# The scan of a gated linear-attention layer on one core: first inverse with swapped sides, one centred output, channel sums moved

## What is computed

```python
def step(S, inp):
    d_t, k_t, v_t, kk_t, a_t = inp[:5]
    sa = jnp.einsum("bhvk,bhk->bhv", S, -kk_t)
    S = (S * d_t[:, :, None, :] + sa[..., None] * (kk_t * a_t)[:, :, None, :]
         + v_t[..., None] * k_t[:, :, None, :])
    out = jnp.einsum("bhvk,bhk->bhv", S, inp[5]) if emit else None
    return S, out
...
kk = kk * lax.rsqrt(jnp.sum(kk * kk, axis=-1, keepdims=True) + 1e-12)
...
o = (o - mean) * lax.rsqrt(var + GN_EPS)
o = o * ln_g + ln_b
bonus = jnp.sum(r * k_sum * r_k, axis=-1, keepdims=True) * v
y = (o + bonus) * jax.nn.silu(g)
```

## Time and profile before

| | |
|---|---|
| median of 3 runs | 2918.58 us (2914.32 to 2923.76) |
| the profiled execution | 2924.89 us |
| its span, mean clock of TensorE | 2923.1 us, 0.95 |
| PE busy in the span | 2625.3 us, 90% |
| the scan within the span | about 1118 to 1830 us |
| a pair of steps in the middle of the scan | 80.6 to 87.4 us |

### The profile page before, as it was taken

One profiled execution on the slowest core, in us unless ns is written; L12 is line 12 of the kernel. 1 busy time (PEld: TensorE's weight loads), 2 busy tenths in 40 slices (PEclk: granted clock), 3 DMA queues, 4 the chain that ended last, 5 costly groups with the idle time before them and its releaser, 6 DMA issues. The chain is left out here.

```text
span 2923.1 us, 66756 instructions
## 1 busy us (share of the span) xinstructions
PE 2625.3 (90%) x28836; PEld 2002.2 (68%) x28836; DVE 1514.2 (52%) x2665; ACT 1133.3 (39%) x1779; POOL 748.4 (26%) x436
## 2 busy tenths in 40 slices
PE   7998899979899996888888887989999999898987
PEld 5776588747678785777777776767788655476745
DVE  4734578883652213545555554334540366515995
ACT  4633332242452433444444443234422344423333
POOL 2423200002212125545544440112223200041201
PEclk9999899999789897999999999989999999998998
DMA  4224344233444431111111100542312100144431
GB/s 153 87 72 134 134 112 127 69 122 113 161 151 146 173 137 57 42 47 47 44 45 53 40 5 25 207 151 65 115 58 80 58 1 1 53 136 141 136 89 58
DMA packets 83663, 266.38 MB, mean 91 GB/s; under 512 B 11824, under 2 KB 12848, under 8 KB 82992
## 3 DMA queue, kind: packets, MB, share of 16 engines
q1 hardware_dynamic: 74160, 236.97, 25.4%
q10 hardware_dynamic: 9216, 25.17, 2.2%
HBM read 203.04 MB, written 36.70 MB: 82 GB/s over the span
## 5 line engine op out<-in xcount | busy, mean ns | idle before, releaser
L373 PE MATMUL ps<-h_parts_conv,w_parts_one 128*128 128x512 f32 x3168 | 581.0, 344 | 16.1 <-DVE h_parts_conv L359 13.6
L373 PEld LDWEIGHTS ps<-h_parts_conv,w_parts_one 128*128 128x128 f32 x3168 | 496.1, 191 | 105.4 <-DVE h_parts_conv L359 15.9
L373 PE MATMUL ps<-scratch_scan 64*64 64x64 f32 (+1 forms) x15936 | 371.4, 233 | 85.2 <-issue 47.9
L373 PEld LDWEIGHTS ps<-scratch_scan 64*64 64x64 f32 x15936 | 332.6, 135 | 130.3 <-issue 99.1
L441 POOL TENSOR_TENSOR w_parts_rwkv_out<-ring,w_parts_rwkv_out 128x1024 fp32r<-128x1024 f32 x78 | 186.4, 2391 | 788.5 <-ACT w_parts_rwkv_out L370 788.5
L441 POOL TENSOR_TENSOR w_parts_one<-ring,w_parts_one 128x1024 fp32r<-128x1024 f32 x82 | 207.3, 2529 | 679.6 <-ACT w_parts_one L370 679.4
L370 ACT ACTIVATE scratch_scan<-ps 128x384 f32<-128x384 f32 x560 | 241.2, 493 | 346.2 <-PE ps L373 201.0
L367 DVE SCALAR_TENSOR_TENSOR scratch_conv<-scratch_conv,vec 128x256 f32<-128x256 f32 (+1 forms) x656 | 330.2, 578 | 0.2
L373 PE MATMUL ps<-h_parts_attn,w_parts_rwkv_out 128*128 128x512 f32 (+1 forms) x1536 | 328.6, 373 | 0.0
L373 PEld LDWEIGHTS ps<-h_parts_attn,w_parts_rwkv_out 128*128 128x128 f32 x1536 | 264.0, 189 | 58.1 <-issue 10.2
L370 ACT ACTIVATE w_parts_rwkv_out<-ring 128x1024 fp32r<-128x1024 f32 x104 | 109.6, 1056 | 368.2 <-PE ps L373 340.9
(11 more groups left out here) (218 smaller groups left out, 3368.0 us busy)
## 6 DMA issues: line engine op xcount, KB each, us to landing
ring<-in_weights SPq DMA_DIRECT2D x311, 512.0 KB, 3.8
rwkv_spill<-scratch_conv ACTq DMA_DIRECT2D x64, 384.0 KB, 2.3
stream<-rwkv_spill SPq DMA_DIRECT2D x64, 384.0 KB, 3.7
scratch_conv<-scratch_conv SPq DMA_DIRECT2D x128, 103.1 KB, 2.2
scratch_conv<-scratch_conv SPq DMA_DIRECT2D x128, 67.4 KB, 2.0
x_spill<-stream SPq DMA_DIRECT2D x2, 3072.0 KB, 11.6
y_spill<-scratch_scan SPq DMA_DIRECT2D x8, 384.0 KB, 2.8
scratch_rwkv_out<-y_spill SPq DMA_DIRECT2D x8, 384.0 KB, 6.4
```

Of the source, the lines that this page charges most:

```text
L373: return nc.tensor.matmul(o, l, r, start=start, stop=stop)
```

## The change

- A is made with swapped sides: `first_inverse(w)` forms the 64x64 products anew from AR and XX, 24 products that use all four pairings of partition halves, into the banks of both halves h at once. The identity is no longer added on PE. `p_start` multiplies by one of two triangular masks and then adds the identity in two more DVE instructions; these signal `p_started`, on which P(0), T(0) and `inverse_update` now wait.
- RD is gone. ACT copies RC into YT (two copies) and squares from there (two squares), `out_square`; it first waits for the store of YT of the pair before (`y_out`). `normal_out` is one multiply of YT in SBUF.
- PE's order: BO goes between WU(1) and Q(0); RC (even steps) and KS (odd steps) between NP and Q(1); RS behind VT. FILLS is written anew to match.
- DVE: `bonus_values` goes from behind link 7 to behind `decayed_a`. ACT: `kk_square` and its logarithms go to either side of the copies of T(1), `out_square` behind them, `out_log` and `out_inverse_root` ahead of the copies of T(3).

```diff
-            def first_inverse(w, e):
-                for n in range(6):
-                    pe.wait_ge(*read_at("G", w, n))
-                room_for(pe, "A", w, e)
-                o = bank3(fill_bank("A", w, e))
-                for par in range(2):
-                    mm(o[HS[par]], idh(par), identb[HS[par]], True, False)
-                for j in pairs_of(e):
-                    for h in range(2):
-                        for par in range(2):
-                            last = mm(o[HS[par], 2 * (j - 3 * e) + h, :], XX[HS[par], aa_plane(w), j, 0, h, :], idh(par),
-                                      False, (j, h) == (3 * e + 2, 1))
-                last.then_inc(*done_inc("A", w, e))
+            def first_inverse(w):
+                for h in range(2):
+                    room_for(pe, "A", w, h)
+                o = [bank3(fill_bank("A", w, h)) for h in range(2)]
+                for j in range(HALFC):
+                    for par in range(2):
+                        for h in range(2):
+                            last = mm(o[h][HS[par], j, :], AR[w % 3][HS[h], 2 * j + par, 0, :], XX[HS[h], bk_plane(w), j, 0, par, :])
+                            if (j, par) == (HALFC - 1, 1):
+                                last.then_inc(*done_inc("A", w, h))
...
             def p_start(w):
+                for h in range(2):
+                    v.wait_ge(*done_at("A", w, h))
+                    vtt(PQ[w % 2][:, h::2, :], bank3(fill_bank("A", w, h)), first_mask(w % 2)).then_inc(*read_inc("A", w, h))
+                for h in range(2):
+                    v.wait_ge(*read_at("A", w, h))
+                    vtt(PQ[w % 2][:, h::2, :], PQ[w % 2][:, h::2, :], identb, ALU.add).then_inc(p_started, 1)
+
+            def normal_out(i):
+                v.wait_ge(rt_ready, i + 1)
+                vtt(YT, YT, RT).then_inc(gained, 1)
...
+            def out_square(i):
+                if i > 0:
+                    a.wait_ge(y_out, 16 * i)
+                for e in range(2):
+                    a.wait_ge(*done_at("RC", i, e))
+                    act(YT[:, cols(e)], PS[:, fill_bank("RC", i, e) * 512:fill_bank("RC", i, e) * 512 + HALFC * CH],
+                        ACT.Copy).then_inc(*read_inc("RC", i, e))
+                for e in range(2):
+                    a.wait_ge(*read_at("RC", i, e))
+                    act(SQ[:, cols(e)], YT[:, cols(e)], ACT.Square).then_inc(out_squared, 1)
...
                 T(0)
                 at(w_and_u, "WU", p, 1)
+                both(bonus_sums, "BO")
                 Q(0)
...
                 at(own_values, "NP", p)
+                both(centred, "RC")
+                both(kk_sums, "KS")
                 Q(1)
```

More of the change, by code:

```diff
@@ L1918, in inv_t @@
                 if lv == 0:
-                    for h in range(2):
-                        pe.wait_ge(*read_at("A", w, h))
+                    pe.wait_ge(p_started, 2 * (w + 1))
                 if n > 2:
@@ L2084, in scan_tensor @@
                 both(values, "VT")
-                both(kk_sums, "KS")
+                both(square_sums, "RS")
                 chain(p, 5)
@@ L2092, in scan_tensor @@
                 chain(p, 7)
-                both(centred("RC"), "RC")
-                both(bonus_sums, "BO")
                 both(p_turned(4), "P4")
@@ L2104, in scan_tensor @@
                 both(p_turned(0), "PI")
-                both(centred("RD"), "RD")
                 at(outputs, "O", p)
@@ L2206, in inverse_update @@
                     if lv == 0:
-                        for e in range(2):
-                            v.wait_ge(*read_at("A", w, e))
+                        v.wait_ge(p_started, 2 * (w + 1))
                     else:
@@ L2252, in scan_vector @@
                     decayed_a(w1)
+                if one and w1 % 2 == 1:
+                    for e in range(2):
+                        bonus_values(w1 // 2, e)
                 if three:
@@ L2286, in scan_vector @@
                     next_state(w3, 7)
-                if one and w1 % 2 == 1:
-                    for e in range(2):
-                        bonus_values(w1 // 2, e)
                 if three:
@@ L2301, in scan_vector @@
                     cumulate(wc)
-                if fill_unit("RD", p - 1) is not None:
-                    finish_out(fill_unit("RD", p - 1))
-                if fill_unit("RD", p) is not None:
-                    for e in range(2):
-                        normal_out(fill_unit("RD", p), e)
+                if fill_unit("RC", p - 1) is not None:
+                    finish_out(fill_unit("RC", p - 1))
+                if fill_unit("RC", p) is not None:
+                    normal_out(fill_unit("RC", p))
                 if three and w3 % 2 == 1:
@@ L2386, in bonus_scale @@
                 act(BON, BON, ACT.Identity, scale=BSC[:, i:i + 1], bias=BBI[:, i:i + 1]).then_inc(bon_scaled, 1)
-            def out_square(i, e):
-                a.wait_ge(*done_at("RC", i, e))
-                act(SQ[:, cols(e)], PS[:, fill_bank("RC", i, e) * 512:fill_bank("RC", i, e) * 512 + HALFC * CH],
-                    ACT.Square).then_inc(*read_inc("RC", i, e))
+            def out_square(i):
[5 more added lines that the diff above has]
+                        ACT.Copy).then_inc(*read_inc("RC", i, e))
+                for e in range(2):
+                    a.wait_ge(*read_at("RC", i, e))
+                    act(SQ[:, cols(e)], YT[:, cols(e)], ACT.Square).then_inc(out_squared, 1)
             def out_log(i, e):
@@ L2435, in scan_scalar @@
                     k_factor(wp)
-                T(1)
-                turned(2)
                 if new_pair is not None:
                     kk_square(new_pair)
+                T(1)
+                if read_pair is not None:
+                    out_square(read_pair)
+                if new_pair is not None:
+                    kk_log(new_pair, 0)
+                    kk_log(new_pair, 1)
+                    kk_inverse_root(new_pair)
+                turned(2)
                 T(2)
```

66 lines of the change are left out of this document (23 added, 43 removed), and 8 rows, old and new, of the table FILLS.

## The result

The changed kernel takes 2947.47 us, the median of 4 runs (2943.57 to 2953.17), beside 2916.6 us for the kernel before on the same chip: a ratio of 1.0109, 95% interval 1.0094 to 1.0124. It is about 32 us slower. The forecast was 2895 us, so the sign is wrong. The profiled execution took 2943.57 us and was the fastest of the four, while that of the kernel before, 2924.89 us, was slower than the others of that kernel; so the two traces differ by 18.7 us only, and show somewhat less of each loss than the medians do.

A forecast was written before the change was run, and what follows sets the result against it. PE, busiest but idle 11 us a pair, was taken as looping with DVE's updates in the scan. Terms -0.7 + 2.0 - 3.5 + 0.4 - 0.3 - 0.8 = -2.9 us a pair, -23 in eight: 2895 us, range 2868 to 2910.

The forecast's parts named there:

- one centred output: Odd step, P(5) to P(1): dropping RD's four wide products takes 1.3 us off PE's road.
- the bank wait: Odd step, P(1) to P(2): P(1)'s second half waits until DVE has read BO; +2.0 us, ends 0 and +3.3.
- The SBUF-only additions: DVE after P(4): two identity additions ahead of link 9, taken at 0.47 us each; upper end +1 us.
- P(3) to P(4) at 5.1 us instead of 8.9: Odd step: without KS and BO there, Q(3) starts 2.65 us after P(3) and P(4) at 5.1 us.
- P(4) to P(5): Both steps: first inverse saves PE 1.96 us, but through DVE only about 0.6 (odd) and 0.8 us (even) arrive.
- Covers: Moved sums fill PE idle time: BO before Q(0) net 0.6 us; RC before Q(1) costs 1.3, covers 0.86, net +0.4.
- The slower one: Rival, chance 0.06: out_square waits for YT's late store; 15 us late costs 4 us a pair, 2950 us.
- nothing happens: Rival, chance 0.06: bank wait at +3.3 and additions at +2 leave a gain of 0, 2919 us.
- More comes out: Rival, chance 0.22: PE's work falls 5.2 us a pair and part of the "issue" waits goes; 2850 to 2880 us.
- code supply: Rival, chance 0.09: fetching program code bounds the scan, so only the instruction count matters; 9 us gained, 2910 us.

The follow-up runs named there:

- The filled kernel: The changed kernel plus four wide products of constants, results discarded, in PE's new waits (odd P(1) halves; before link 10 each step): 2942.33 us, ratio 1.0058.
- adds_late: The changed kernel with DVE's two identity additions behind inverse_update(4) and link 10, PI at the end of PE's step: 2933.85 us, ratio 1.0029.
- both waits mended: The changed kernel with bonus_values ahead of inverse_update(0) and the identity additions late, PI at the step's end: 2921.14 us, ratio 0.998.
- bo_forward_adds_late: New inverse, single centred output, additions late, sums at old places except BO, moved before Q(0) and read first on DVE: 2905.92 us, ratio 0.9961.
- the best: The changed kernel with all channel sums at old places, identity additions late, PI at step's end; run twice: ratios 0.992 and 0.9918.
- best_again: Second run, unedited, of the changed kernel with channel sums at old places, additions late and PI at step's end: 2892.57 us, ratio 0.9918.

## Why the prediction was wrong

My sum had three parts in it: the inverse at -0.6 and -0.8 us a pair (-11 us in eight), one centred output at -1.3 (-10 us), and the moves of the sums, the rest, at -0.2 (-2 us). Measured, one added to the other in this order, they are +4, -6 and +34 us. By the table, a pair is 5.7 us over the forecast: 1.9 of it in P(3) to P(5) of the odd step, 1.1 in its P(1) to P(2), 1.5 in the two P(5) to P(1), and the rest in the even step.

Two steps failed. The two additions on DVE were priced by their width alone, and the sum had no term for the clock behind PE's waits. A third, the bank wait, had the right mechanism and too small a size.

**"The SBUF-only additions ... half of the 0.94 of a 756-wide one is 0.47"** is a step that failed. They take 1.08 us on average, 2.02 for the two in the row shown. My upper end was +1 us for the two; the row is 1.1 us over my value. The width itself was nearly right: with one input from PSUM, or beside an idle POOL, such an instruction takes 0.54 to 0.55 us:

```profile
L359 DVE TENSOR_TENSOR scratch_scan<-scratch_scan,con x32: 544/1248/2152, 1142.9 to 1775.9; 128x384 f32<-128x384 f32 x32
```

(shortest, median and longest in ns). What the row could not tell is that in the new place POOL works on SBUF as well. The Trainium skill's page "SBUF — State Buffer", section "Who interferes with whom", says that a VectorE instruction with two SBUF inputs contends with a GpSimd instruction that reads SBUF, and that the later one is blocked. These traces agree: the additions are slow beside POOL's `scratch_scan,con` row, POOL's own instructions take 1.49 us each there (5.94 for four), where all 160 of them have a mean of 1085 ns, and the slowness goes with the second SBUF input. I had used a page of the Trainium skill on TensorE's side and not this one, which spoke against the change. Undoing the collision alone gave back 20 us, moving the additions 23.

**"A bank that is read late": the mechanism is right, the size is not.** P(1) was split as forecast, and the wait was 1.90 us. The part P(1) to P(2) of the odd step grew by 3.1 us instead of 2.0, near my upper end of 3.3. That end was to come from the code wait, and of this 0.77 us did stay (at 1411.12, where I had 1.21 swallowed); the larger part is the clock: MR(1) and T(1) behind the wait take 3.46 us for 129 rows, and 2.63 when the wait is gone.

**No step of mine asked what a wait does to the clock.** This is the failure with the longest reach. The earlier trace rows show 1.00, and I took it as given. The filled kernel puts the price at some 15 us of the 32 by the ratios and at 8 in the scan of the two traces; its own products may cost something too, so the price may be higher. It overlaps with the waits that it follows, so these numbers are not to be added.

**"P(3) to P(4) at 5.1 us instead of 8.9"** came to 6.19 instead of 8.47 (8.90 in the pair that I read): -2.3 of -3.8. Of what is missing, 1.0 us is code waits in the odd step shown, 0.44 and 0.57; the 0.66 stands ahead of P(3):

```profile
1419.88 2.26 PE L373 MATMUL ps<-scratch_scan 64*64 64x64 f32 x106 [0.66 <-issue]
1422.07 0.87 PE L1825 MATMUL ps<-con,scratch_scan 128*128 128x128 f32 x6
...
1423.95 2.72 PE L373 MATMUL ps<-scratch_scan 64*64 64x64 f32 x126 [0.44 <-issue]
...
1427.29 1.55 PE L373 MATMUL ps<-con,scratch_scan 64*64 64x64 f32 x46 [0.57 <-issue]
```

I had given 0.5 us for them in P(3) to P(5). The queue of program code made 93 fetches in the five pairs (95 before), so there was hardly less to bring in.

**P(4) to P(5)**, forecast at -0.6 and -0.8, is +0.7 and -0.6. The inverse itself is as forecast: the row at 1429.75 holds T(4), the first inverse and two links, 104 rows in 1.87 us, so some 0.86 us for the 48 rows of the first inverse, where it took 2.71. The additions and the low clock behind them took the gain in odd steps. In adds_late it is there: -0.75 and -1.54.

**Covers.** I charged BO before Q(0) with 0.6 us and RC before Q(1) with 0.4. Odd P(5) to P(1) came out at -0.1 instead of -0.7, and even P(1) to P(2) at +0.9 instead of +0.4. Even P(5) to P(1), where I had nothing, is +0.9: that part starts with the transposes at half clock.

**The rivals.** The slower one did not happen by its mechanism: in the scan's middle ACT waits for PE alone, never for a store:

```profile
ACT scratch_scan L370 <- PE ps L373: 137.1, 87, 4.7
ACT scratch_scan L370 <- PE ps L1825: 70.1, 27, 6.9
```

The kernel was slower by others, one of which I had as an upper end (+3.3) inside "nothing happens", together with the additions at theirs (+2). Had I kept these two apart as one rival and asked of each how it might be exceeded, 2919 would not have been the end of it. "More comes out" and "code supply" are both refuted by the sign.

**What stays open.** With both waits mended the new places still cost 0.6% (0.998 against 0.992). Of it BO's place is 0.3 to 0.4%. That a wide product before Q(0) delays a loop that has no slack there is a reading that fits odd P(5) to P(1), 10.21 us in bo_forward_adds_late against 9.39 and 9.41 in the two runs of the best; a run of its own was not made for it. It is not all of it: P(1) to P(2) of the odd step grew as well, 10.04 us against 8.84 and 8.76. In that part code waits are 2.6 us a step instead of 1.7 in best_again, and 2.2 us instead of 0.7 are at half clock. So code supply and the clock are a rival to the place itself, and no run parts them. Nor was it measured why the clock of some steps falls and of others not.

## What to carry to other kernels

Where a change puts an idle piece into an engine that was never idle for long, look at the granted clock of the stretch behind it, not only at the length of the wait. Before an elementwise instruction is costed by its width, look at what POOL does at the place it goes to, and whether both inputs lie in SBUF. And when a small instruction is added in front of an update that everything waits for, ask first whether its result is needed there: here it was not, and moving two additions (with the transposes PI that read them) was worth 0.8%, as much as the whole change was meant to bring.

## What was not expected of the hardware

- The granted clock went from 1.00 to 0.51 for 3.4 us behind a stretch of 3.1 us in which PE was busy for 0.76 us. In the kernel before, with waits of PE of up to 1.5 us, the five pairs stayed at 1.00.
- 128x384 fp32 on DVE with both inputs in SBUF: 0.59 to 2.15 us beside an instruction of POOL and 0.54 beside an idle POOL, 1.08 on average; 0.55 us with one input in PSUM at the same place, POOL busy or not.
- Every idle piece of PE over 0.3 us without a releaser ended 1.2 to 1.6 us behind the end of a packet of program code, 38 of 38 in the five pairs before and 28 of 28 after.
- A wait taken away can come back as another: with BO read first, a code wait of 2.63 us stood ahead of 1408.43, in the same part of the step as the bank's 1.90 us, and the low clock was there all the same (1407.96 to 1411.37 us).
